# A two-block transformer kernel, with and without the products between its two routers' steps

## The reference

```python
logits = (t @ w_router).astype(jnp.float32)
top_vals, top_idx = lax.top_k(logits, TOP_K)
top_w = jax.nn.softmax(top_vals, axis=-1)
...
for e in range(N_EXPERTS_2):
    out = out + gates[:, e:e + 1] * swiglu(t, w1[e], w3[e], w2[e])
```

## Time and profile before

| | |
|---|---|
| time before, median of 3 runs | 1798.89 us (1797.91 to 1800.91) |
| the profiled execution, its own time | 1800.01 us |
| its span, first to last instruction | 1798.2 us |
| TensorE busy with matmuls | 1654.1 us, 92% of the span |
| DVE, ACT, POOL busy | 558.5, 196.7, 40.6 us |
| DMA | 548.38 MB, mean 305 GB/s |
| mean granted TensorE clock | 0.976 of full speed |

### The profile page before, as it was taken

The page is one execution under the profiler, slowest core; times in us unless marked ns, Lnnn a source line. Parts: engine busy times, 40 slices in busy tenths (PEclk is TensorE's granted clock), DMA queues, the critical chain, the costliest instruction groups (busy, mean ns, idle before and its releaser), DMA issues.

```text
span 1798.2 us, 23651 instructions
## 1 busy us (share of the span) xinstructions
PE 1654.1 (92%) x10057; PEld 889.5 (49%) x10057; DVE 558.5 (31%) x905; ACT 196.7 (11%) x334; POOL 40.6 (2%) x126
## 2 busy tenths in 40 slices
PE   8989988777899999999999999999999999987778
PEld 6669664343764445448564444454444445332223
DVE  2785542111654667458340100020010002010013
ACT  1352121111121000020210000000000000000001
POOL 5002000000000000000000000000000000000000
PEclk9999999898899999999999999999999999999999
DMA  7032579999763344442579999999999999999990
GB/s 285 4 120 95 212 294 421 422 422 408 275 228 131 138 175 172 156 167 62 200 287 380 420 420 419 419 419 419 414 419 419 420 419 419 419 419 419 420 405 37
DMA packets 109367, 548.38 MB, mean 305 GB/s; under 512 B 11153, under 2 KB 18434, under 8 KB 96466
## 3 DMA queue, kind: packets, MB, share of 16 engines
q1 hardware_dynamic: 106128, 540.68, 74.8%
q0 software_dynamic: 1664, 5.05, 0.7%
q10 hardware_dynamic: 1474, 1.19, 0.3%
HBM read 543.51 MB, written 1.05 MB: 303 GB/s over the span
## 4 chain that ended last, share of the span: by engine, by line
PE 70%; DMA 15%; DVE 8%; SPq 4%; issue 2%; ACT 2%; DVEq 0%; ACTq 0%
PE ps L2234 21%; PE ps L2292 11%; DMA ring<-in_exp_w 7%; PE ps L2085 7%; DMA ring<-in_w_down 7%; PE ps L2148 3%; SPq L911 3%; PE ps L1985 3%; PE ps L1938 3%; PE ps L1877 2%; PE ps L1768 2%; PE ps L2058 2%; PE ps L2023 2%; PE ps L1649 1%; SPq L865 1%
## 5 line engine op out<-in xcount | busy, mean ns | idle before, releaser
L2234 PE MATMUL ps<-ring,xT 128*64 128x448 f32 (+2 forms) x2336 | 450.7, 540 | 23.5 <-DMA ring<-in_exp_w 21.0
L2234 PEld LDWEIGHTS ps<-ring,xT 128*64 128x64 f32 (+2 forms) x2336 | 187.6, 137 | 284.7 <-issue 282.2
L2292 PE MATMUL ps<-ring,work 128*32 128x512 f32 (+5 forms) x1120 | 208.0, 546 | 14.4 <-DMA ring<-in_exp_w 14.4
L3247 DVE TENSOR_TENSOR work<-work,ps 128x448 f32<-128x448 f32 x40 | 34.3, 919 | 493.6 <-PE ps L2234 493.6
L2292 PEld LDWEIGHTS ps<-ring,work 128*32 128x32 f32 (+2 forms) x1120 | 84.8, 135 | 131.8 <-issue 125.9
L1938 PE MATMUL ps<-xT,ring 128*128 128x256 f32 x384 | 86.0, 388 | 0.0
L1938 PEld LDWEIGHTS ps<-xT,ring 128*128 128x128 f32 x384 | 74.6, 195 | 10.6
L2085 PE MATMUL ps<-ring,xT 128*128 128x512 f32 (+1 forms) x192 | 78.9, 557 | 0.3 <-ACT xT L1290 0.3
L1855 PE MATMUL ps<-ring,work 128*32 128x256 f32 x944 | 59.5, 406 | 19.0 <-DMA ring<-in_w_up 17.9
L1393 ACT ACTIVATE work<-ps 128x448 f32<-128x448 f32 x40 | 21.8, 544 | 445.7 <-PE ps L2234 445.0
L2991 DVE SCALAR_TENSOR_TENSOR work<-work,c_sb 128x256 f32<-128x256 f32 x120 | 58.2, 485 | 4.3
(11 more groups left out here) (556 smaller groups left out, 1732.7 us busy)
## 6 DMA issues: line engine op xcount, KB each, us to landing
ring<-in_exp_w SPq DMA_DIRECT2D x346, 896.0 KB, 17.7
work<-in_exp_w SPq DMA_DIRECT2D x38, 896.0 KB, 18.3
ring<-in_w_down SPq DMA_DIRECT2D x32, 1024.0 KB, 17.2
ring<-in_w_up SPq DMA_DIRECT2D x31, 1024.0 KB, 18.8
ring<-in_w_gate SPq DMA_DIRECT2D x28, 1024.0 KB, 16.9
ring<-in_dense_w SPq DMA_DIRECT2D x13, 2048.0 KB, 11.3
ring<-in_w_in SPq DMA_DIRECT2D x6, 2048.0 KB, 12.1
ring<-in_w_in SPq DMA_DIRECT2D x8, 1104.0 KB, 15.0
```

The source lines that it names most:

```text
L2234: ins = mm(ps[at:at + width, b, 0:RUN_BLOCK], run_x(r)[:, k, at:at + width], w[m][:, b * RUN_BLOCK:(b + 1) * RUN_BLOCK], start=(k == 0), s ...
L2292: ins = mm(ps[at:at + width, bank + n0 // 512, n0 % 512:n0 % 512 + n], turned[:, c * P + at:c * P + at + width], w[m][:, at0 - RUN_PIECE * ...
```

## The change

All 19 products go, in both routers. Nothing else is changed: every wait, every other product and every instruction of the other engines stays.

```diff
-            def keep_warm(n, bank):
-
-                for _ in range(n):
-                    mm(ps[:, bank, 0:2 * P], before[:, :], x_sb[:, 0, 0:2 * P], start=True, stop=True)
-
...
             m1p.raise_by(logits(7, 1, 8 + E1, w_both), "logits 1")
-            keep_warm(8, 2)
             pe.wait_ge(*m1d("mask"))
             places(m1p, E1)
-            keep_warm(2, 2)
...
             turn_tile(x_sb, bp, "xT ffn 1", 0, [bd("ln1 1 0")])
             pe.wait_ge(*ba("xT ffn 1 1"))
             logits(4, 0, E2, w_router)
-            keep_warm(3, 3)
             turn_tile(x_sb, bp, "xT ffn 1", 1, [bd("ln1 1 1")])
             pe.wait_ge(*ba("xT ffn 1 3"))
             bp.raise_by(logits(5, 1, E2, w_router), "logits")
-            keep_warm(4, 3)
             pe.wait_ge(*bd("mask"))
             places(bp, E2)
-            keep_warm(2, 3)
```

## The result

The kernel without the products takes 1803.37 us (median of 20 runs, 1798.13 to 1806.27), the kernel before 1799.98 us (20 runs, 1796.34 to 1803.58): a ratio of 1.0021, 95% interval 1.0014 to 1.0028. It is slower, by 0.21%. Forecast were 1803.5 us and 0.26% slower, with a range of 1798.6 to 1807.3.

What follows compares the result with a forecast made beforehand. The experts are paced by DMA and both routers lie on the path in full; losses of 1.4 us in the first router and 3.25 in the second, rounded to 4.6, on the median 1798.89 gave 1803.5 us, range 1798.6 to 1807.3.

Steps and rivals of the forecast that it cites:

- Both routers lie on the path: Both routers: a microsecond gained or lost ahead of 245.56 or 919.75 moves the weight stream behind it and the end.
- The wait for the removed products is saved: Both routers: `places` starts at the mask, no longer behind removed products; 1.1 us gained in the first, 0.65 in the second.
- `places` at half clock: Both routers: the 10 records of `places` slow down; 0.9 us lost in the first, 0.4 us in the second.
- The second router's transposes and logits: Second router: 8 transposes wholly at half clock lose 0.3 us, the second tile's 16 logits records 1.6 us.
- The gathers: Gather of each router: 16 of 32 records at half clock, 1.6 us lost in each.
- The upper bound of 3.2: Each gather: all 32 records at half clock to the end, 3.2 us lost; 7.9 us in all for both routers.
- Nothing else should move: Outside the routers: removed products read resident data and issue no DMA, so a later restart only lengthens the transfers' pause.
- The price for throttling: Both routers, by the skill's rule: half of 17 us added half clock, less 1.75 gained; 6.8 us lost, 1805.7 us.
- The waits alone: Rival, both routers: clock no lower than now, only the in-order delay goes; 1.75 us faster, 1797.1 us, chance 0.07.
- The partial case: Rival, both routers: one larger half-clock term goes; loss 0 to 3.6 us, typically 2.2, 1801.1 us, chance 0.33.
- The late return: Rival: both gathers at half clock to their ends; 7.8 us slower in all, 1806.7 us, chance 0.12.

Runs made afterwards that it cites:

- 8 columns each: All 19 products of the kernel before stay, but with 8 columns each instead of 256; 1803.92 us, ratio 1.0023.
- 12 for 8 products: The kernel before with 12 products instead of 8 ahead of the first router's `places`; 1800.12 us, ratio 0.9998.
- none in 1, filled in 2: Against the kernel before, no products in the first router, and products also in the second router's pauses; 1794.21 us, ratio 0.9971.
- the run with fewer products: The kernel before with 6 products for 8 ahead of the first router's mask and 3 for 4 ahead of the second's; 1799.13 us, ratio 0.9985.
- the one with products ahead of the mixer: The kernel before with 12 products of 128 columns added in the pause behind block one's last scatter, ahead of the first mixer; 1799.64 us, ratio 1.0001.

## Why the prediction was right, point by point

The direction and the mechanism in the routers were right. That the size fits is luck in part: there are two misses of opposite sign, 4.3 us too little for the routers by the profiles, and a stream 4.7 us shorter that had no term.

- *Both routers lie on the path.* From SP's first transfer behind the second router to the end all profiles of the change and of before take 874.3 to 875.0 us, and with 8 columns each the first router's 4.2 us are not made up in the stream behind it (255.09 us, as before). Right by the profiles; the run with 12 for 8 products (0.9998) does not bear it out.
- *The wait for the removed products is saved.* `places` starts at 236.67, right at the mask (236.62); in the second router at 912.49 with the mask at 912.43. 1.1 and 0.65 us gained, as forecast.
- *`places` at half clock.* First router: 2.45 us from its start to DVE's next step instead of 1.53, 0.9 lost, as forecast. Second: 2.42 instead of 2.06, 0.4 lost, as forecast.
- *The second router's transposes and logits.* 1.97 us instead of 1.64, and 3.58 instead of 1.95: 0.3 and 1.6 lost, as forecast.
- *The gathers* are the term that was too small. I took 16 of 32 records at half clock, 1.6 us for each gather, because the removed products had run some 4 us until the clock rose. The gathers take 6.65 and 6.71 us, 2.8 and 2.9 us more: the clock rose about 6 us into each (246.1 and 922.0), and 28 or more records had run at half. The upper bound of 3.2 was the better guess here. In the three profiles that have the changed first router with another second one, the gather takes 5.25 to 5.88 us, 1.4 to 2.0 us more, as forecast.
- *The first router's second logits* had no term. I let the drop fall at 233.4 as in the profile; in both profiles of the change it came at 229, in the pause ahead of these logits, and took them from 1.98 to 3.64 us: 1.7 more. Sums: 1.7 - 1.1 + 0.9 + 2.8 = 4.3 us against 1.4 forecast, and 0.3 + 1.6 - 0.6 + 0.4 + 2.9 = 4.6 against 3.25. With the same program up to there, the kernel without router one's products has these logits at 1.98 and 2.91 us, and "none in 1, filled in 2" at 1.98; their first routers lose 1.45, 2.8 and 1.2 us. So the 1.4 us forecast is what two of five profiles show, and what it left open is where the drop falls, which differs between executions.
- *"Nothing else should move"* was wrong. I had looked at data, DMAs and waits, not at where the 20 records and their weight loads stood in TensorE's stream of instructions. The prediction named the sign of this itself, another time of the stream from its first transfer on. Without the products the stop at 458.14 is gone, and the stream is 4.7 us shorter. Against 8.9 us in the routers and 1.7 in the middle (where the change has a drop at 666 that before lacks) that leaves 5.9 us; up to the first router and at the end another 1.2 us differ, so that the spans are 4.7 us apart. The medians say 3.4 and 1.3.
- *The price for throttling.* The added half clock is 13.7 us in each router (17.1 for 3.4, 20.5 for 6.8). By the rule of the Trainium skill, "TensorE: Matmul & The Clock Gate", section "Terms", an estimate from that is 13.7 us in all, less 1.75 gained, 11.9; measured are 8.9. The rows say why: from 233.0 to 236.7 and from 910.6 to 912.5 TensorE was at half clock and did nothing.
- *The rivals.* The waits alone: out, `places` starts earlier and the kernel is slower. The run with fewer products (0.9985) may hold its gain, and does not show it by itself. The partial case had its grounds in executions that differ, and they are borne out: before and the change each repeat their stages within 0.3 us, but another kernel shows an unedited first router 1.4 us off, and the changed first router lost from 1.2 to 4.3 us in five profiles. The late return is what the gathers did in both profiles of the change; the 7.8 us of this case would have been passed, by 8.9, but for the stream.
- *The chances.* One sum is wrong: 0.45, 0.12 and 0.03 make 0.60 for slower by over 0.2%, not 0.57. The 0.55 that was taken lies 0.05 below the sum of its own cases.

The kernel without router one's products has a middle of 397.19 us once and of 394.01 once. About half of that is a drop of the clock, at 660.9 in the first profile and absent in the second: all eight profiles with a drop between 660 and 680 have a middle of 397.2 to 398.7 us, all six without one 394.0 to 395.9. The other half, and what the changed instructions have to do with where the drops fall, stay open.

## What to carry to other kernels

Products that keep TensorE's clock are worth their time where the unbroken work behind them is on the path, and their worth is read from that work's own length at half and at full clock; put them in every pause, and few enough that the awaited step finds the queue empty. Here that was worth 0.4%, though a drop can fall in a filled router all the same, and no products in the first router with filled pauses in the second did about as well (0.9971). Then judge an edit by stages as well as by its total: adding or removing instructions on an engine shifts all that follows in its stream, and here the loss of a stop 200 us behind the edit, with the half clock around it, gave back half of what the edit cost. A variant that gains without a reason in the edited stage deserves a control and a table of stages before it is believed or thrown away.

## What the runs showed of the hardware that was not expected

- A stop of 1.8 to 3.2 us in TensorE's stream that stays at one number of instructions from the start, two records earlier for every product (two records) added ahead, in nine profiles of eight kernels, always behind 4109 matmul records and always ending 1.3 to 1.5 us behind the end of a 16 KB transfer of instructions; not seen in five profiles of three kernels, where that place falls among large products and the transfer had ended before.
- Matmuls of 8 columns with their weight loads, back to back for 3.31 of 3.40 us, did not bring the clock back from 1.2 GHz here; in the kernel before and in the one with products ahead of the mixer it came back while those of 256 columns ran.
- The gathers of the change ran for 5.9 and 6.1 us at 1.2 GHz until 2.4 GHz was granted, the removed products of the kernel before for about 4.
- One and the same TensorE program up to the second router gave first routers of 24.12 to 27.17 us in five profiles, by where the drop of the clock fell in it.
